# Twelve eight-row transfers in the last expert weight load of a two-block kernel

## The reference, cut to what matters

```python
def moe_expert_choice(h, router_w, w_gate, w_up, w_down):
    ...
    gate, idx = lax.top_k(jnp.swapaxes(aff, 1, 2), cap)      # 16 experts, 32 tokens each
    xs = h[bidx, idx]
    hid = jax.nn.silu(jnp.einsum('becd,edf->becf', xs, w_gate)) * jnp.einsum('becd,edf->becf', xs, w_up)
    ye = jnp.einsum('becf,efd->becd', hid, w_down) * gate[..., None].astype(h.dtype)
    return jnp.zeros_like(h).at[bidx, idx].add(ye)

def second_block(x, ...):
    h = rms_norm(x, norm_mix_g[i])
    proj = jnp.einsum('bsd,dc->bsc', h, w_in[i])
    ...
```

## Time and profile before

| | us |
|---|---|
| median of 3 runs | 1532.93 |
| lowest, highest | 1532.58, 1533.30 |
| the profiled execution's own time | 1532.63 |
| its span in the trace | 1530.8 |

### The profile page before, as it was taken

One profiled execution on the slowest core, in us unless ns is written; L12 is line 12 of the kernel. 1 busy time (PEld: TensorE's weight loads), 2 busy tenths in 40 slices (PEclk: granted clock), 3 DMA queues, 4 the chain that ended last, 5 costly groups with the idle time before them and its releaser, 6 DMA issues.

```text
span 1530.8 us, 18705 instructions
## 1 busy us (share of the span) xinstructions
PE 1195.3 (78%) x8200; PEld 750.6 (49%) x8200; DVE 562.5 (37%) x832; ACT 424.7 (28%) x554; POOL 31.9 (2%) x36
## 2 busy tenths in 40 slices
PE   5999999998665666656656556666656899999998
PEld 2878899943221211212212112212212689999997
DVE  5887776511110101101101101101101597777566
ACT  3766555231000000000000000000000454367545
POOL 0011000000000000000000000000000000000000
PEclk9999999999878877778777878778877999999999
DMA  9746769799999999999999999999999845565551
GB/s 347 249 153 248 275 246 328 273 424 436 428 434 428 435 429 431 431 430 432 430 433 429 433 430 433 428 435 428 433 427 429 295 160 172 159 193 191 180 183 54
DMA packets 109968, 520.92 MB, mean 340 GB/s; under 512 B 6064, under 2 KB 85936, under 8 KB 93632
## 3 DMA queue, kind: packets, MB, share of 16 engines
q1 hardware_dynamic: 109744, 519.63, 84.3%
q10 hardware_dynamic: 144, 0.09, 0.0%
HBM read 518.66 MB, written 1.05 MB: 340 GB/s over the span
## 4 chain that ended last, share of the span: by engine, by line
PE 48%; DMA 47%; SPq 2%; DVE 2%; ACT 1%; issue 1%; DVEq 0%
PE B L1747 16%; DMA four<-in_wd 15%; DMA four<-in_wu 15%; DMA four<-in_wg 13%; PE B L2221 7%; PE B L1755 6%; PE B L2264 3%; PE B L1759 3%; DMA wslot<-in_w_in 2%; PE B L1916 2%; PE B L1904 1%; PE B L1727 1%; PE B L2178 1%; PE B L1919 1%; DMA wslot<-in_w_out 1%
## 5 line engine op out<-in xcount | busy, mean ns | idle before, releaser
L2221 PE MATMUL B<-four,xs 128*32 128x512 f32 x1824 | 290.5, 794 | 191.9 <-DMA four<-in_wu 134.4
L2221 PEld LDWEIGHTS B<-four,xs 128*32 128x32 f32 x1824 | 72.3, 140 | 389.9 <-issue 313.8
L2264 PE MATMUL B<-four,hidT 128*32 128x512 f32 x896 | 156.8, 864 | 99.2 <-DMA four<-in_wd 98.5
L2264 PEld LDWEIGHTS B<-four,hidT 128*32 128x32 f32 x896 | 38.6, 150 | 206.1 <-issue 131.4
L1747 PE MATMUL B<-hnh,whj 128*128 128x256 f32 x488 | 138.4, 284 | 0.0
L1747 PE MATMUL B<-hnh,wslot_r 128*128 128x256 f32 x488 | 137.7, 282 | 0.0
L1747 PE MATMUL B<-hn_r,whj 128*128 128x256 f32 x488 | 137.3, 281 | 0.0
L1002 DVE TENSOR_TENSOR wslot_r<-wslot,whj 128x2048 fp32r<-128x2048 f32 x52 | 118.8, 2289 | 31.1 <-ACT whj L537 31.0
L537 ACT ACTIVATE whj<-wslot 128x2048 fp32r<-128x2048 f32 x51 | 97.2, 1913 | 87.6 <-PE B L1747 82.0
L1372 DVE COPY ye<-B 128x512 f32<-128x512 f32 x15 | 10.4, 692 | 282.1 <-PE B L2264 282.1
L1341 DVE SCALAR_TENSOR_TENSOR x<-B,mod,x 128x256 f32<-128x256 f32 x128 | 55.9, 480 | 149.8 <-PE B L2196 149.8
(11 more groups left out here) (518 smaller groups left out, 1958.9 us busy)
## 6 DMA issues: line engine op xcount, KB each, us to landing
four<-in_wu SPq DMA_DIRECT2D x29, 4096.0 KB, 33.3
four<-in_wd SPq DMA_DIRECT2D x28, 4096.0 KB, 33.8
four<-in_wg SPq DMA_DIRECT2D x28, 4096.0 KB, 33.4
wslot<-in_w_in SPq DMA_DIRECT2D x58, 1024.0 KB, 5.2
aslot<-in_ada_w SPq DMA_DIRECT2D x16, 1024.0 KB, 7.3
pair<-in_wg SPq DMA_DIRECT2D x7, 2048.0 KB, 13.1
pair<-in_wu SPq DMA_DIRECT2D x6, 2048.0 KB, 11.9
pair<-in_wd SPq DMA_DIRECT2D x5, 2048.0 KB, 20.6
```

The lines of the kernel that those rows point to most:

```text
L2221: mm = e.matmul(B[b][32 * j:32 * j + 32, :], tokens, columns(t, j), start=k == 0, stop=k == 7)
L2264: mm = e.matmul(B[3 + db][32 * r:32 * r + 32, :], hidT[:, 128 * c + 32 * j:128 * c + 32 * j + 32], v2(tile_at_page(t + c // 2))[:, c % 2, ...
```

## The change

The first tile of the last pair is loaded as before. Of the second, rows 96 to 127 go out as one transfer on the semaphore that the whole tile had before, and rows 0 to 95 as twelve transfers of eight rows each, on one new semaphore. TensorE waits for both ahead of the second four products.

```diff
@@ -383,6 +383,7 @@
         l_tail = [signal(f"l_tail{i}", 16) for i in range(4)]
+        l_rows = signal("l_last_rows", 16)
@@ -451,7 +452,10 @@
                     e.dma_start(homes[n, r][:, 0:SLOT], expert_src(t, 2)[:, 0:SLOT]).then_inc(*l_last())
-                    e.dma_start(homes[n, r][:, SLOT:2 * SLOT], expert_src(t, 2)[:, SLOT:2 * SLOT]).then_inc(*landed[r]("expert", t + 1))
+                    e.dma_start(homes[n, r][96:128, SLOT:2 * SLOT], expert_src(t, 2)[96:128, SLOT:2 * SLOT]).then_inc(*landed[r]("expert", t + 1))
+                    for i in range(12):
+                        rows = slice(8 * i, 8 * i + 8)
+                        e.dma_start(homes[n, r][rows, SLOT:2 * SLOT], expert_src(t, 2)[rows, SLOT:2 * SLOT]).then_inc(*l_rows(i))
                     return
@@ -2257,6 +2261,8 @@
                             e.wait_ge(*(landed[tile_page(t)].at("expert", t + 1) if i else l_last.at()))
+                            if i:
+                                e.wait_ge(*l_rows.at(11))
```

## The result

| | before | changed |
|---|---|---|
| median, us | 1532.93 (1532.58 to 1533.30, 5 runs) | 1539.82 (1539.44 to 1541.23, 5 runs) |
| profiled execution, its span | 1532.63, 1530.8 | 1539.62, 1537.8 |

The ratio is 1.0046, 95% interval 1.0035 to 1.0056: the change makes the kernel 6.9 us slower. Forecast were 1531.9 and a range of 1531.0 to 1535.0.

A forecast was written before the change was run, and what follows sets the result against it. The last expert bytes' landing at the block border was taken to bound the kernel; 1532.63 us less 1.06 of TensorE idle time gave 1531.57, plus 0.30 for the median 1531.87, forecast 1531.9, range 1531.0 to 1535.0.

The forecast's parts named there:

- What bounds the kernel: Border between the blocks: each microsecond the last expert bytes move reaches the end; two paths lie within a few tenths.
- How the engines stand: Around 1195 us: about half of the 16 DMA engines a tile ahead, the others some 5 us of rows behind.
- (a): Line 454's tile: on the engines not carrying the small transfers, expert rows end 6 x 0.32 = 1.93 us sooner.
- (b): Line 454's tile: on the eight engines carrying the small transfers, expert rows end 1.93 us later.
- (c): If the eight engines are those ahead: last landing 1199.70, last four products start at 1200.65, gain 1.06 us.
- rival B: The eight engines include ones behind: line 454's tile and W0 land 1.93 us later, 1534.9 us; chance 0.25.
- W0: The tile after line 454, landing at 1204.41 before; forecast near 1202.5, or 1206.34 if the eight include engines behind.
- (d): Second block: later tiles land sooner too, worth nothing, since TensorE is the bound there.
- (f): TensorE's wait ahead of the second four products: the extra semaphore costs 0.
- (e): SP's issue: twelve more transfers take 5.4 us, moving W0's issue to 1184.7, hidden behind the queue.
- (g): Completion of twelve more transfers on an engine: 0 to 2.2 us each, taken as 0.
- The upper rival: Each small transfer pays 2.2 us, the twelve 26 us from 1195: kernel up to 1553 us; chance 0.07.

The follow-up runs named there:

- section 5: SP waits ahead of line 453 until the tiles before have landed: kernel before 1539.02 us, changed kernel 1545.08, rows 0 to 95 as one transfer 1541.05.
- section 6: Load groups behind the kernel before's last store: three 128-row tiles 9.9 us, second split 32 and 96 rows 12.1; both behind four eight-row transfers 15.0 and 19.1.
- section 7: Kernel before plus 512 KB behind line 454: 128 rows 1534.02 us, eights four apart 1536.47, eights side by side 1539.68, one of rows 0 to 63 1539.84.
- section 3: Kernel before with line 454's tile split: by columns 1532.73 us; only the last 2 KB by rows 1534.42; rows 64 to 127 and 0 to 63 1540.80.
- the column split: Kernel before with line 454's tile as two transfers of all 128 rows, first 2 KB and last 6 KB of each row: 1532.73 us, ratio 1.0000.
- one of 64: Kernel before plus 512 KB behind line 454 as one transfer of rows 0 to 63: 1539.84 us, ratio 1.0044.
- the extra bytes: 512 KB more behind line 454 of the kernel before; as eight transfers of eight rows, four apart 1536.47 us, side by side 1539.68.
- sections 1 to 3 and 7: Section 1: changed kernel, rows four apart in both memories 1541.45 us, HBM only 1541.62, SBUF only 1540.13; section 2: rows 0 to 95 as one transfer 1539.31.
- the probe: Load groups behind the kernel before's last store, behind four eight-row transfers: three 128-row tiles 15.0 us, second split into 32 and 96 rows 19.1.
- own-rows kernel: Kernel before plus 512 KB behind line 454 as eight transfers of eight rows four apart, rows 0 to 63: 1536.47 us, ratio 1.0021.

## Why the prediction was wrong

**What bounds the kernel: right.** The border of the blocks passed every microsecond on: 7.1 us later there, 7.0 us more span. Both paths moved together, by 7.1 and 6.9.

**How the engines stand: not contradicted, and I drew the wrong conclusion.** I used the two groups, some 5 us apart, only for who has how many rows left. That they are apart goes with about half of the price of a row split: last products 6.7 us later in the queue as it is, 3.3 in step (section 5), 4.1 against 2.2 us behind the kernel (section 6). That the eight engines might all be of the group ahead does not hold by section 7: the latest of them is 0.7 to 1.35 us ahead of the last engine, not some 5.

**(a), (b): the step that failed.** "6 x 0.32 us sooner" holds that a row costs 0.32 us for whichever engine carries it, and that what one engine carries is nothing to another. 0.32 was measured on transfers of 128 rows only. In the changed kernel a row of 8 KB took 0.47 us in the mean of both tiles, and the packets of the other loads slowed down with them: 224 to 255 GB/s at a DMA share near 1 for 15 us, and tiles ahead 3.5 and 4.9 us late. So the expert rows did not end 1.93 us sooner: the last 8 KB packet starts at 1207.6, in the kernel before at 1200.8, and the last four products, which (c) has at 1200.65, start at 1208.82. No rival held this. The Trainium skill did: the port table of SBUF — State Buffer ("Door 1: The DMA port swizzle") with the map of engines of DMA: Bandwidth & Descriptors ("The descriptor swizzle") says that rows 0 to 7 are not the rows of eight engines, and under "Rules for kernel authors" stands that instead of two transfers to halves of the partitions one should use one of 128. Its reason there is that they serialize; the runs show more than that, 7.7 us for 1 MB in two halves (section 3). The prediction takes from the second page how many engines a transfer uses, and not where they write.

**(c): wrong in size and in sign.** Its 1.06 us gain needed the latest of the eight to be over 1.9 us ahead. By section 7 it was 0.7 to 1.35 ahead, so that without any disturbance the tile would have landed 0.6 to 1.2 us later. This is rival B with a smaller price than its 1.93, and a tenth or two of what happened. The sign that I had named for B, 3 us idle ahead of the last four products, is there (2.67) and misleads: it stands behind 3.4 us of delay in the products before (1200.05 instead of 1196.65). The other sign, W0 at 1206.3, is not there (1211.3).

**(d), (f): right**, as far as anything shows it: the second block is busy for 308.39 us as before, and the column split has a second semaphore and costs 0.0 us (ratio 0.9990 to 1.0009).

**(e): right.** Twelve issues took 4.06 us (5.4 estimated), and W0's wait stayed behind the queue.

**(g): the term was small, its lower end was near.** One transfer of 96 rows and twelve of eight differ by 0.5 us, inside the scatter of either, so one transfer more costs some 0.05 us in the full queue, and with the scatter at most some 0.2. The upper rival, 26 us, would have needed what twelve do not cost even alone (11.0). The estimate of 11.4 us beside it is near what they take alone, and not what they cost in the queue. Its 0.95 us stands in the Trainium skill's table (DMA: Bandwidth & Descriptors, "Bandwidth") for transfers of 128 partitions issued from GpSimd, not for ones from SP.

**The range and the chances.** 1535.0 left out every price between 2 us and 20. "Slower by more than can be told from no change" had a chance of 0.10, and for other reasons than the one that the runs show. The bounds of (g), 0 to 2.2 us for each transfer, spanned the result, and I kept them out of the range by an argument about the queue that said nothing on shapes the trace did not hold.

**What stays open.** Shown is that a split by rows, with the same bytes, makes the packets of all loads around it slow, and one by columns does not. That the ports of SBUF are the place is inferred from shapes; no run reads a port, and from section 3 on the rows in HBM and in SBUF were changed together, so that the reading side is not excluded. The size is not explained: with half of the rows at other engines than in a transfer of 128 (two halves, one of 64, rows four apart in the change), the price is as high as with nearly all of them. That may be why rows four apart do not help inside the change, though they help alone and in the extra bytes; it is argued, not shown. And no run tells why half of the engines are behind. No version beat the kernel before; the column split equals it.

## What to carry to other kernels

Split a load by columns, not by rows, if a full queue stands before it: all 128 rows twice cost nothing here, 32 and 96 rows 6.3 us. A price per row read from one shape of transfer says nothing about another shape, and when transfers ahead of an edit land later while the DMA share stays near 1 and the GB/s fall, look at how long one packet takes: here it rose from 0.31 us to 0.47. Moving rows from one engine to another changes more than the count of rows that each carries.

## What the runs showed of the hardware

- **Packets of 8 KB take 0.31 us each while the queue is full, with next to no scatter, as long as every transfer has all 128 rows** (256 of 256 in the kernel before between 309 and 321 ns), and 0.33 to 0.50 in the mean, up to 0.97 for one, with a transfer of fewer rows near them (sections 1 to 3 and 7). The exception is eight rows four apart behind whole tiles: 320 of 320 took 309 to 324 ns.
- **A transfer can delay those ahead of it in its queue**, by 3.5 and 4.9 us in the changed kernel, and by 2.5 in the probe. The Trainium skill has a case of the kind (DMA: Bandwidth & Descriptors, "Back-pressure in remote DMA"): a saturated port of SBUF clogs the path back to the engines. It speaks there of writes between cores; here there was one core, loading from HBM.
- **Draining the queue once cost 5.8 us**: 1539.02 against the 1533.25 of the kernel before, measured along with it. From 1190 to 1200 us, across the wait, the DMA share is 0.49 and 0.48 in windows of 5 us, instead of 1.02 and 0.91.
- **Rows four apart take SP longer to issue**: twelve transfers of eight rows side by side took SP 4.00 us to issue, with rows four apart 7.97.
- **The same idle time left TensorE at different clocks.** After 2.39 us of it the last four products took 1.07 us, the time they take at 2.4 GHz, and the granted clock stood at 1.00 from 1200 to 1205; after 2.27 us, in the own-rows kernel, they took 1.78:

```profile
1200.00:1205.00 5.00, 2.73 (x19) 0.48 (x18) 0.00 (x0) 0.00 (x0) 0.00 (x0) 0.88 0.96 313
1205.00:1210.00 5.00, 5.00 (x25) 4.37 (x22) 2.30 (x6) 2.92 (x6) 0.00 (x0) 0.78 1.09 357
```

The windows are those of the own-rows kernel; the second is at 0.78, between 1.2 and 2.4 GHz, while TensorE is busy all the time. Ahead of both idle times stood another of 1.91 us, in both kernels. Of 2.1 us between the two spans (1534.2 and 1532.1), the last four products and the `keep_on` products behind them account for 0.7 and 0.9.
